# The MLP's products by one level of Strassen's method, after a mixer that runs first for all blocks

## What is computed

```python
h = rmsnorm(x, norm_mix_g)
z = gelu(h @ w_in);  u, v = split(z, 2);  v = rmsnorm(v, v_g)     # w_in 1024 x 2048
s = causal 128x128 mixing of v per chunk of 128 tokens and per group of 128 channels, + b_s
x = x + (u * s) @ w_out                                             # w_out 1024 x 1024
a = relu(rmsnorm(x, norm_mlp_g) @ w1)                               # w1 1024 x 4096
x = x + (a * a) @ w2                                                # w2 4096 x 1024
out = rmsnorm(x, final_g)
```

## Time and profile before

| | us | share of the span |
|---|---|---|
| median of three runs | 2017.19 | |
| span of the profiled execution | 2014.1 | |
| TensorE matmuls (9097) | 1994.1 | 99% |
| weight loads into TensorE | 1661.2 | 82% |
| VectorE (939 instructions) | 910.8 | 45% |
| ScalarE (745) | 668.1 | 33% |
| GpSimd (105) | 43.5 | 2% |
| DMA, 212.24 MB | | mean 105 GB/s |

### The profile page before, as it was taken

One profiled execution on the slowest core, in us unless ns is written; L12 is line 12 of the kernel. 1 busy time (PEld: TensorE's weight loads), 2 busy tenths in 40 slices (PEclk: granted clock), 3 DMA queues, 4 the chain that ended last, 5 costly groups with the idle time before them and its releaser, 6 DMA issues.

```text
span 2014.1 us, 22400 instructions
## 1 busy us (share of the span) xinstructions
PE 1994.1 (99%) x9097; PEld 1661.2 (82%) x9097; DVE 910.8 (45%) x939; ACT 668.1 (33%) x745; POOL 43.5 (2%) x105
## 2 busy tenths in 40 slices
PE   7999999999999999999999999999999999999998
PEld 6888888888888888888888888888888888888887
DVE  4345345444525445444533545444453444444435
ACT  5424233223443333222334243222243425222222
POOL 1000000000000000000000000000000000000000
PEclk9999999999999999999999999999999999999999
DMA  6222322324432322322342222323335222323321
GB/s 240 84 84 84 105 89 98 104 85 145 168 105 65 103 90 99 104 84 103 131 183 97 71 89 99 104 84 104 104 126 182 91 83 85 104 84 103 102 85 63
DMA packets 101085, 212.24 MB, mean 105 GB/s; under 512 B 3464, under 2 KB 4512, under 8 KB 101024
## 3 DMA queue, kind: packets, MB, share of 16 engines
q1 hardware_dynamic: 100976, 211.30, 31.1%
q10 hardware_dynamic: 48, 0.01, 0.0%
HBM read 202.91 MB, written 8.39 MB: 105 GB/s over the span
## 4 chain that ended last, share of the span: by engine, by line
PE 99%; DVE 0%; DMA 0%; ACT 0%; SPq 0%; POOL 0%; issue 0%; POOLq 0%; ACTq 0%
PE bank L671 91%; PE bank L748 4%; PE bank L712 2%; PE bank L699 1%; DMA xin<-in_x 0%; DVE hT_lo L496 0%; ACT hT_hi L392 0%; DVE w_lo L489 0%; ACT junk L374 0%; ACT w_hi L351 0%; DVE x L559 0%; SPq L294 0%; DVE xin L503 0%; DVE x L552 0%; POOLq L164 0%
## 5 line engine op out<-in xcount | busy, mean ns | idle before, releaser
L489 DVE TENSOR_TENSOR w_lo<-w_raw,w_hi 128x2048 fp32r<-128x2048 f32 x176 | 401.3, 2286 | 299.4 <-ACT w_hi L351 299.4
L351 ACT ACTIVATE w_hi<-w_raw 128x2048 fp32r<-128x2048 f32 x176 | 336.1, 1915 | 474.2 <-DMA w_raw<-in_mlp_w 449.4
L671 PE MATMUL bank<-w_hi,a_hi 128*128 128x512 f32 x1024 | 398.9, 390 | 0.0
L671 PE MATMUL bank<-x1T_hi,w_hi 128*128 128x512 f32 x1024 | 398.7, 389 | 0.0
L671 PE MATMUL bank<-w_hi,a_lo 128*128 128x512 f32 x1024 | 398.4, 389 | 0.0
L671 PE MATMUL bank<-x1T_hi,w_lo 128*128 128x512 f32 x1024 | 398.4, 389 | 0.0
L671 PE MATMUL bank<-x1T_lo,w_hi 128*128 128x512 f32 x1024 | 398.4, 389 | 0.0
L671 PE MATMUL bank<-w_lo,a_hi 128*128 128x512 f32 x1024 | 398.4, 389 | 0.0
L552 DVE SCALAR_TENSOR_TENSOR x<-bank,x_r,x 128x512 f32<-128x512 f32 x256 | 179.1, 751 | 184.6 <-PE bank L671 184.6
L540 DVE TENSOR_TENSOR relu_a<-relu_a 128x512 f32<-128x512 f32 x128 | 79.9, 686 | 394.3 <-ACT a_hi L405 394.3
L671 PEld LDWEIGHTS bank<-w_hi,a_lo 128*128 128x128 f32 x1024 | 192.2, 188 | 40.0
(11 more groups left out here) (79 smaller groups left out, 1666.8 us busy)
## 6 DMA issues: line engine op xcount, KB each, us to landing
w_raw<-in_mlp_w SPq DMA_DIRECT2D x128, 1024.0 KB, 5.3
w_raw<-in_a_w_in SPq DMA_DIRECT2D x32, 1024.0 KB, 5.0
w_raw<-in_a_w_out SPq DMA_DIRECT2D x16, 1024.0 KB, 5.0
xin<-in_x SPq DMA_DIRECT2D x16, 512.0 KB, 7.8
x<-in_x SPq DMA_DIRECT2D x4, 2048.0 KB, 7.9
out<-x SPq DMA_DIRECT2D x16, 512.0 KB, 4.4
ws_raw<-in_a_w_s SPq DMA_DIRECT2D x1, 512.0 KB, 10.0
bias_rows<-in_a_b_s SPq DMA_DIRECT2D x1, 512.0 KB, 11.4
```

The lines of the kernel that those rows point to most:

```text
L351: act.activation(w_hi[slot_of(h)][:, :, :], w_raw[slot_of(h)][:, :, :], ACT.Copy)\
L489: dve.tensor_tensor(w_lo[slot_of(h)][:, :, :], w_raw[slot_of(h)][:, :, :], f32(w_hi[slot_of(h)][:, :, :]), ALU.subtract).then_inc(w_ready, 1)
L671: ins = pe.matmul(BANK[s][j][:, :], stationary(x_part, k, j), moving(y_part, k, j), start=first and k == 0 and n == 0, stop=final and k == ...
```

## The change

The mixer runs first for all four blocks, then the MLP for all tokens. The MLP works on two pairs of blocks (1024 tokens) and four chunks of 1024 hidden columns. Each of its products of a pair and a chunk is a 2 x 2 product of quadrants of 512 (for the first product; 1024 x 1024 by 1024 x 1024) and is made from seven quadrant products (`STEPS`) in place of eight, by Strassen's method in Winograd's form. There are 2 x 4 such products with w1 (`UP`) and as many with w2, 16 in all: 112 steps (`LAST`) of 48 matmuls.

- **Operands.** Every step has a weight and a data operand of 1 MB; both are loaded, split on ScalarE and split on VectorE, in four slots each, two steps ahead. A step's loads wait for the products of the step four before.
- **Sums of quadrants** are made once and kept in DRAM. GpSimd has 40 jobs (`add_up`), each: load four tiles of 128x512 (1 MB), four adds in a row, store 1 MB. 16 jobs are for w1, 16 for w2, 8 for the normed activations. 20 run in the mixer, five per block around the norms; two per chunk, in chunks 2 to 5 three, in the MLP's first half. GpSimd issues their DMAs itself.
- **Combinations of products.** A step that continues a sum adds into the same bank without a start; others are copied to SBUF by ScalarE (`keep_bank`) or added there by VectorE (`add_bank`). TensorE waits for the reader of the bank two steps before (`bank_free`). In the first half `finish_first` (relu and square on ScalarE) and `finish_second` (six pieces on VectorE) make the seven operands of the second product for each of four column tiles of a chunk, in one of two buffers `sums`; GpSimd stores each (seven tiles, 1.8 MB) to `a2s`, and ScalarE waits for the store before it writes the buffer again.
- **Activations.** The norm of x1 is applied before the transposes (a new tile `x1n`), which go to DRAM (`xs`), and x1 itself goes to DRAM (`x1s`). Transposes of the next input move into the output units of the mixer. In the second half the residual is loaded back (`Y`), and VectorE adds each bank to it.
- **End.** The first pair is normed and stored during the second pair's steps; the second pair's eight row tiles after the last add.
- The instruction streams are written out without loops.

Added, and the core of what goes ("..." for what is left out):

```diff
-    with pe.Fori(0, PAIRS) as i:
-        h = Turn(i, LOOP0)
-        mlp_added(b, i * 16 - 4)
-        group_up(b, h, 1)
-        pe.wait_ge(a2_ready, b * M1S + i * 8 + 4)
-        mlp_added(b, i * 16)
-        token_major(a2[0], b, h + 2, 0, True, True)
...
-    def add_mlp(b, h, half, s, tiles=range(TT)):
-        for t in tiles:
-            dve.wait_ge(products, bank_value(b, h, t))
-            rows = x1[:, t, half * N:(half + 1) * N]
-            dve.scalar_tensor_tensor(out=rows, in0=BANK[s][t][:, :], scalar=x1_r2[:, t:t + 1],
-                                     in1=rows, op0=ALU.mult, op1=ALU.add)\
-                .then_inc(x1_mlp_done, 1)
...
+STEPS = 7
...
+wsum = nc.dram_tensor("wsum", [2 * CHUNKS, P, 4, KU * N], F32, kind="Internal").ap()
+xs = nc.dram_tensor("xs", [PAIRS, P, 8, KU * N], F32, kind="Internal").ap()
+a2s = nc.dram_tensor("a2s", [UP, P, STEPS, KU * N], F32, kind="Internal").ap()
+x1s = nc.dram_tensor("x1s", [BLOCKS, P, TT, D], F32, kind="Internal").ap()
...
+def banks_read(g, j, by_act):
+    n = sum(4 for i in range(g) if read_by_act(i) == by_act)
+    return n + j + 1
+def read_by_act(g):
+    return g < UP * STEPS and g % STEPS in (0, 2, 3, 6)
+jobs = w1_jobs[:15] + s_jobs[0] + w1_jobs[15:] + s_jobs[1] + w2_jobs
...
+    def data_operand(g):
+        n, i = g // STEPS, g % STEPS
+        op = ACT_OPERAND[i]
+        if g >= SLOTS:
+            sp.wait_ge(products, done(FIRST + g - SLOTS))
+        elif g < 2:
+            sp.wait_ge(mix_done, BLOCKS * G)
+        else:
+            sp.wait_ge(products, done(FIRST - 1))
+        if n < UP:
+            b = n // CHUNKS
+            if op < S2:
+                sp.wait_ge(x1T_stored, 16 * 4 * (b + 1))
+            else:
+                sp.wait_ge(job_stored, sums_stored("s", b))
+            src = xs[b][:, op, :]
+        else:
+            for s in range(2):
+                sp.wait_ge(a2_stored[s], 16 * 2 * (n - UP + 1))
+            src = a2s[n - UP][:, i, :]
+        sp.dma_start(a_raw[g % SLOTS][:, :, :], src.rearrange("p (k f) -> p k f", f=N))\
+            .then_inc(a_loaded[g % SLOTS], 16)
...
+        else:
+            for g in range(2):
+                weight_operand(g)
+                data_operand(g)
+            weight_operand(2)
+        sp.wait_ge(x1_attn, (q + 1) * 2 * TT)
+        sp.dma_start(x1s[q], x1[:, :, :]).then_inc(x1_stored, 16)
+        if q < BLOCKS - 1:
+            sp.wait_ge(x1_stored, 16 * (q + 1))
+            sp.wait_ge(x1n_ready, (q + 1) * TT)
+            sp.dma_start(x1[:, :, :], x_v[q + 1]).then_inc(x1_loaded, 16)
...
+    def add_up(n):
+        kind, index, k = jobs[n]
+        if n:
+            pool.wait_ge(job_stored, 16 * n)
+        if kind == "w":
+            src = (w1_v[index] if index < CHUNKS else w2_v[index - CHUNKS])[:, :, k, :]
+            pool.dma_start(job[:, :, :].rearrange("p (h f) n -> p h (f n)", h=2), src)\
+                .then_inc(job_loaded, 16)
+        else:
+            pool.wait_ge(x1T_stored, 16 * 4 * (index + 1))
+            pool.dma_start(job[:, :, :], xs[index][:, 0:4, k * N:(k + 1) * N]).then_inc(job_loaded, 16)
+        pool.wait_ge(job_loaded, 16 * (n + 1))
+        q0, q1, q2, q3 = (job[:, i, :] for i in range(4))
+        s = 4 * n
+        if kind == "w":
+            pool.tensor_tensor(q3, q3, q1, ALU.subtract).then_inc(job_step, 1)
...
+            pool.wait_ge(job_step, s + 3)
+            pool.tensor_tensor(q2, q2, q0, ALU.subtract).then_inc(job_step, 1)
...
+        pool.wait_ge(job_step, s + 4)
+        to = wsum[index][:, :, k * N:(k + 1) * N] if kind == "w" else xs[index][:, 4:8, k * N:(k + 1) * N]
+        pool.dma_start(to, job[:, :, :]).then_inc(job_stored, 16)
...
+    for q in range(BLOCKS):
+        next_jobs(2)
+        rstd(v_sq, v_squares(q), v_ms, v_ms_done, v_rstd, v_rstd_done, q)
+        next_jobs(1)
+        if q < BLOCKS - 1:
+            rstd(x_sq, x_squares(q + 1), x_ms, x_ms_done, x_rstd, x_rstd_done, q + 1)
+        next_jobs(2)
+        rstd(x1_sq, x1_squares(q), x1_ms, x1_ms_done, x1_rstd, x1_rstd_done, q)
+    for c in range(UP):
+        next_jobs(3 if 2 <= c < 6 else 2)
+        for j in range(KU):
+            pool.wait_ge(second_half, 6 * (KU * c + j + 1))
+            pool.wait_ge(first_half, 4 * (KU * c + j + 1))
+            pool.dma_start(a2s[c].rearrange("p i (k f) -> p i k f", f=N)[:, :, j, :],
+                           sums[j % 2][:, :, :]).then_inc(a2_stored[j % 2], 16)
+    every = 16 * 2 * UP
+    pool.dma_start(Y[0][:, 0:TT, :], x1s[0]).then_inc(Y_loaded[0], 16)
+    pool.wait_ge(a2_stored[0], every)
+    pool.dma_start(Y[0][:, TT:2 * TT, :], x1s[1]).then_inc(Y_loaded[1], 16)
+    pool.dma_start(final_g_rows[:, :], final_g.partition_broadcast(P)).then_inc(final_g_loaded, 16)
+    pool.dma_start(Y[1][:, 0:TT, :], x1s[2]).then_inc(Y_loaded[2], 16)
+    pool.wait_ge(a2_stored[1], every)
+    pool.dma_start(Y[1][:, TT:2 * TT, :], x1s[3]).then_inc(Y_loaded[3], 16)
...
+    def keep_x1T(q, half):
...
+        act.wait_ge(x1T_copied, q * KD + 4 * half + 4)
+        op = 2 * (q % 2) + half
+        act.dma_start(xs[q // 2][:, op, :].rearrange("p (k f) -> p k f", f=N),
+                      x1T[q][:, 4 * half:4 * half + 4, :]).then_inc(x1T_stored, 16)
...
+    def keep_bank(g, j, to, func=ACT.Copy):
+        act.wait_ge(products, done(FIRST + g, j))
+        act.activation(to, BANK[g % 2][j][:, :], func).then_inc(act_read, 1)
+    def finish_first(c, j):
+        f = 4 * (KU * c + j)
+        if KU * c + j >= 2:
+            act.wait_ge(a2_stored[j % 2], 16 * (2 * c + j // 2))
+        elif j == 1:
+            act.wait_ge(x1T_stored, 16 * 2 * BLOCKS)
+        act.wait_ge(dve_read, banks_read(c * STEPS + 5, j, False))
+        act.activation(c11[:, j, :], c11[:, j, :], ACT.Relu).then_inc(first_half, 1)
+        act.activation(c12[:, j, :], c12[:, j, :], ACT.Relu).then_inc(first_half, 1)
...
+    def ahead(g, which):
+        if g + 2 < LAST:
+            if which:
+                split_a(g + 2)
+            else:
+                split_w(FIRST + g + 2)
...
+    for g in range(LAST):
+        c, i = g // STEPS, g % STEPS
+        up = c < UP
+        ahead(g, 0)
+        if g == 1:
+            keep_x1T(BLOCKS - 1, 0)
+        if g == 3:
+            keep_x1T(BLOCKS - 1, 1)
+            act.wait_ge(x1_stored, 16 * BLOCKS)
+        if i == 0 and 0 < c <= UP:
+            finish_first(c - 1, 2)
+            if up:
+                act.wait_ge(first_half, 4 * (KU * (c - 1) + 3))
+                keep_bank(g, 0, c11[:, 0, :])
+            ahead(g, 1)
+            finish_first(c - 1, 3)
+            if up:
+                act.wait_ge(first_half, 4 * KU * c)
+                for j in range(1, KU):
+                    keep_bank(g, j, c11[:, j, :])
+        elif up and i in (0, 2, 3):
+            to = {0: c11, 2: c12, 3: c22}[i]
+            if i == 3 and c:
+                act.wait_ge(second_half, 6 * KU * c)
+            keep_bank(g, 0, to[:, 0, :])
+            ahead(g, 1)
+            for j in range(1, KU):
+                keep_bank(g, j, to[:, j, :])
+        elif up and i == 6:
+            for j in range(KU):
+                if c:
+                    act.wait_ge(second_half, 6 * KU * c)
+                keep_bank(g, j, r21[:, j, :], ACT.Relu)
+                if j < 2:
+                    finish_first(c, j)
+                if j == 0:
+                    ahead(g, 1)
+        else:
+            ahead(g, 1)
...
+    def add_bank(g, j, rows):
+        dve.wait_ge(products, done(FIRST + g, j))
+        dve.tensor_tensor(rows, BANK[g % 2][j][:, :], rows, ALU.add).then_inc(dve_read, 1)
+    def finish_second(c, j):
...
+        dve.wait_ge(act_read, banks_read(g + 6, j, True))
+        dve.tensor_tensor(a21, a21, a21, ALU.mult).then_inc(second_half, 1)
+        dve.wait_ge(first_half, 4 * m + 4)
+        dve.wait_ge(dve_read, banks_read(g + 4, j, False))
+        dve.scalar_tensor_tensor(out=a22, in0=c22[:, j, :], scalar=0.0, in1=c22[:, j, :],
+                                 op0=ALU.max, op1=ALU.mult).then_inc(second_half, 1)
...
+        dve.wait_ge(second_half, f + 5)
+        dve.tensor_tensor(s4, a12, s2, ALU.subtract).then_inc(second_half, 1)
...
+    for g in range(LAST):
+        c, i = g // STEPS, g % STEPS
+        ahead(g, 0)
+        if c < UP:
+            if i == 0 and c:
+                finish_second(c - 1, 2)
+            if i == 1 and c:
+                finish_second(c - 1, 3)
+            if i == 6:
+                finish_second(c, 0)
+            if i in (1, 4, 5):
+                to = {1: c11, 4: c22, 5: c12}[i]
+                for j in range(KU):
+                    dve.wait_ge(act_read, banks_read({1: g - 1, 4: g - 1, 5: g - 3}[i], j, True))
+                    add_bank(g, j, to[:, j, :])
+                    if j == 0:
+                        ahead(g, 1)
+            else:
+                ahead(g, 1)
+            if i == 6:
+                finish_second(c, 1)
+        else:
```

(98 more changed lines are left out.)

801 lines of the change are left out of this document (358 added, 443 removed).

## The result

The changed kernel takes 2035.43 us in the median of four runs (2034.21 to 2038.24), the kernel before 2016.76 beside it: a ratio of 1.0095 with a 95% interval of 1.0083 to 1.0108, so 0.95% slower. I had forecast 1947 and a range up to 2035; the sign was wrong, and the measured time lies just outside the range. The profiled execution has a span of 2036.5 us.

What follows compares the result with a forecast made beforehand. TensorE, busy 1994.1 of 2014.1 us, was taken to bound the kernel. 2014.1 - 174.1 + 4.6 + 3 + 70 + 9 + 10 + 7 = 1943.6 of span, so 1947 us, range 1862 to 2035.

Steps and rivals of the forecast that it cites:

- rival (d): Matmuls continuing an old bank sum, or shorter bank waits, cost 1% on the 112 steps, 12 us: 1959; chance 0.04.
- The chain: MLP's first half: TensorE waits for splits, behind ScalarE's `finish_first`, behind GpSimd's sums stores, at step 2 or 3, chunks 3 to 6.
- rival (b): First MLP half: dearer job and longer window, rounds of 89 and 116 us, slower than before at 2092; chance 0.16.
- The job phase: GpSimd's part of a first-half round before its sums stores: 21 us a job, plus 4.6 for a load queued behind a store.
- The window: GpSimd's four sums stores per chunk, first to last: store 3 at 25.5 us, on a 7.3 us landing of 1.8 MB.
- A round of two jobs is 72 and costs nothing.: First MLP half: GpSimd's round of 30 + 21n takes 72 us with two jobs, against 76.2 of TensorE's work.
- the term of 70 us: Sum of TensorE's losses to GpSimd's rounds over the chunks of the MLP's first half.
- The change of halves: Between the MLP's halves: residual reloaded behind the last sums store, VectorE's first add at 31, bank due at 21.8; 10 us.
- The clock: TensorE's lower granted clock after four stalls of over 10 us: 9 us, bounds 0 and 12.
- The gates: Mixer: the next input's transposes wait for all eight gates, 1.5 us x 3 = 4.6 (0 to 12).
- Start and end: MLP start: third operand's late loads, 3 us; end: eight scalings behind the last add, +7.
- j near 25: j is the time of one GpSimd job, taken as 21 us; at 25 the first half's stalls sum to 142 us.

Runs made afterwards that it cites:

- e3_no_adds: The changed kernel without the four adds of every GpSimd job, whose load and store stay; 1964.17 us.
- e6_sp_early: The changed kernel with sums stores issued by SyncE, store 0 early, the residual's first reload waiting for less, the next input's first transposes one unit later; 1936.54 us.

## Why the prediction was wrong

- **The matmuls.** Right: 8329 of them, 227.4 ns apart in the second half; rival (d) is out.
- **The chain.** Right, and named before: GpSimd's round, `finish_first`, ScalarE's banks and splits, TensorE, with the stalls at step 2 or 3; but they sit in chunks 1 to 7, not 3 to 6. It came out as rival (b), a dearer job and window, which was given 0.16. (b)'s 89 us for a round of two jobs is what was measured, its 116 for three was not (96 to 102.5), and so its time of 2092 was too high.
- **Three jobs.** The job phase was put at 67.6 us with the queued store; chunk 3 has 65.1 (953.88 to 1018.94), chunks 2, 4 and 5 have 75.6, 72.8 and 66.2. Sized about right. A job is not a constant, though: an add takes GpSimd 1.28 us where nothing disturbs it and 3.36 beside VectorE's work (rows of the result); in the jobs on weights the four adds average 1.64 to 1.87, where I had 1.29 + 0.6.
- **The window, the step that failed most.** Put at 25.5 us on a landing of 7.3, from loads that were alone. Measured: 31.0 in chunk 3 (1018.94 to 1049.95) and 35.4 in chunk 6 (1301.58 to 1336.97), with landings of 17.45 and 21.84; over all chunks 26.9 to 35.4. Over chunks 1 to 6 the windows are 34 us longer than put, the job phases 25. Two stores of 1.8 MB go out together behind the last job's 1 MB on the same queue, while SyncE's loads take their share; I had queued none of this ahead of them.
- **"A round of two jobs is 72 and costs nothing."** Wrong: 90.7, 89.1 and 82.0 us in chunks 1, 6 and 7, where TensorE's work is 76.2. I priced job and window once, from quiet rows, for both kinds of round. A job in a round of two takes 26.5 to 27.7 us, in a round of three 21.7 to 25.2 (53.7 us for the two of chunk 6, where 46.6 were put). A likely reason, which no run isolates, is that TensorE stands longer in the rounds of three, so fewer loads and splits run beside the jobs. All rounds bind, and the term of 70 us measures 109.4.
- **The change of halves.** 10 us put, 28.5 measured. The reload behind the store took the 13 us that were put. But piece 3 ended 36 us into the half (which starts at 1382.46), not 18: the jobs of chunk 7 held the first store until 1390.04, and the last one went 28 us behind it, at 1418.22.
- **The clock.** 9 us put (four stalls of 2.3), 28.0 from the granted clock. Fourteen stalls are followed by work at the lower level, three in the mixer and eleven from the MLP's start on, 2.0 us each, so the price was about right and the count wrong.
- **The gates.** 4.6 us put, 13.0 measured. My 1.5 us per block is what e3_no_adds shows (4.7 in three waits); the rest goes with the adds. The rows are below.
- **Start and end.** 3 and 7 us put, 5.2 and 6.9 measured.
- **The range.** Its upper end of 2035 was built from a dearer job alone (j near 25), without a longer window. Adding a window of 31 to 35 us to it, for which the queue's contents spoke, would have put the likeliest time at some 1980 to 2005 (an estimate from the prediction's own rounds), with the sign open.

VectorE through the gates of the first block of after, whose last gate was at 127.81 in the earlier trace rows (start, length, what):

```profile
119.84 0.68 DVE L670 TENSOR_TENSOR yT_lo<-uT,yT_hi 128x512 fp32r<-128x512 f32 x1
...
122.43 2.29 DVE L627 TENSOR_TENSOR w_lo<-w_raw,w_hi 128x2048 fp32r<-128x2048 f32 x1
...
126.34 1.78 DVE L670 TENSOR_TENSOR yT_lo<-uT,yT_hi 128x512 fp32r<-128x512 f32 x1
128.05 0.74 DVE L659 SCALAR_TENSOR_TENSOR biased<-bank,gains,bias_rows 128x512 f32<-128x512 f32 x1
128.82 0.98 DVE L665 TENSOR_TENSOR uT<-uT,biased 128x512 f32<-128x512 f32 x1
129.72 1.75 DVE L670 TENSOR_TENSOR yT_lo<-uT,yT_hi 128x512 fp32r<-128x512 f32 x1
```

GpSimd in the same stretch:

```profile
116.61 0.72 POOL L347 DMA_DIRECT2D job<-in_mlp_w  x1 [5.51 <-DMA wsum<-job]
122.45 3.42 POOL L356 TENSOR_TENSOR job<-job 128x512 f32<-128x512 f32 x1 [5.12 <-DMA job<-in_mlp_w]
125.95 1.63 POOL L358 TENSOR_TENSOR job<-job 128x512 f32<-128x512 f32 x1
```

The same split of y takes 0.68 us with GpSimd idle and 1.75 to 1.78 while a job's adds run, and an add takes 1.63 beside it, or 3.42 where it overlaps a large split (122.43); and in e3_no_adds, where only the adds are gone, the gates stall TensorE 4.7 us in place of 13.0. The gate itself, which reads its first operand from PSUM, keeps its 0.74. The Trainium skill's rule ("SBUF — State Buffer", "Who interferes with whom") is that, outside VectorE's two-port modes, only a VectorE instruction with two SBUF inputs contends with one of GpSimd that reads SBUF, and by that rule the trace agrees. I had cited it for GpSimd's cost only and forgot that VectorE pays the same, on a path that TensorE waits for.

What stays open: in e6_sp_early 8 us of a chunk are read off the chain as VectorE held up by adds, but no kernel here takes the adds away there and leaves the landing of 13 us; and no run says what makes a landing of 1.8 MB take 9.2 to 17.2 us without jobs, the loads or the neighbouring store.

## What to carry to other kernels

When work is moved to an idle engine, write down its whole in-order round, its own DMAs in the order of their queue included, and price it in the busy state in which it has to fit, since prices from quiet rows make just the critical case look hidden. A producer with two buffers is bound by the return time of a buffer, and a store that frees one should not stand behind work that could be anywhere else. A method that saves arithmetic on the bound engine pays only when its side work has room: here the same 40 jobs and the same stores take 2035.4 us in one order and, spread, on two queues and with three smaller waits removed, 1882.0.

## What the runs showed of the hardware

A transfer of 1 MB that GpSimd issues takes its queue 0.7 to 0.9 us to issue; in the loaded stage its load takes 9 to 16 us to land and its store 4.6 to 11, where SyncE's loads of the same size have medians of 4.9 to 8.9 in this kernel and had 5.1 before. The sums store of 1.8 MB lands in 9.6 to 21.8 us in the chain of the changed kernel and in 9.2 to 17.2 without jobs. 42 MB of copies for which nobody waits change 1924.2 us to 1925.5. In a stall of 24 us TensorE is granted 0.50 of its clock, 0.66 in the first 5 us of work behind it and 1.00 in the 10 after. Each of the eight stalls of 6.9 us and more from the MLP's start on is followed by work at the lower level; of the seven short ones three are (2.5 to 3.8 us) and four aren't (1.4 to 2.9 us). A VectorE operation of 128x512 with two SBUF inputs takes 0.68 us alone and, beside GpSimd's adds, 1.67 to 1.79 (0.98 in one of the rows); one that reads PSUM keeps 0.74.
